# Hybrid attention and retention layer on one core: the row factor of the norm applied after the projections, the turned x split as it is, and two weight panels split twice

## The chip, the cores and the metric

The kernel runs on one core of one Trainium2 chip. Its time is the device time of one execution in microseconds (us), and the figure for a kernel is the median of several executions.

## The reference

One residual layer over x of 2048 rows by 1024 columns: a root-mean-square norm of each row, one input projection whose columns go to window attention and to retention (each with its own gate), one output projection, and the residual.

```
def rms_norm(x, g):
    y = xf * lax.rsqrt(jnp.mean(xf * xf, axis=-1, keepdims=True) + EPS) * g
...
q = rms_norm(q, q_gain); k = rms_norm(k, k_gain)         # window attention, 16 heads, 4 key heads of 64
scores = einsum('bnqhgd,bnkhd->bnhgqk', qb, kb) * scale  # 64 queries, 128 keys, ALiBi bias, sink in the softmax
...
a = einsum('bnihd,bnjhd->bnhij', qc, kc) * dmat          # retention: decay inside a chunk of 64
r = g_chunk * r + s_i                                    # and a state from chunk to chunk
o = (o - mu) * lax.rsqrt(var + EPS)                      # norm of each of 8 heads, then a gain
...
out = x + concat(attn * silu(a_gate), ret * silu(r_gate)) @ w_out
```

The row factor of the first norm, 1/sqrt(mean(x*x) + eps), is one number for each row of x. So it may be multiplied into x before the projections or into their results behind them. The norms of q and k don't care for it, except in their eps, and the norm of the retention heads doesn't either if its eps is scaled.

## The kernel before

**Blocks, units, jobs.** The 2048 rows are 4 blocks of 512 (4 tiles of 128). A block has 4 units, one for each group of 4 query heads with their key head and 2 retention heads, so there are 16 units n = 0 to 15. A unit has 20 projection jobs: 0 to 3 make q, k and v of one tile each (384 columns), 4 and 5 the attention gate, 6 and 7 the retention's q and k, 8 to 11 its v and gate, 12 to 19 the output projection, which runs in the middle of the next unit. Every job fills one of three PSUM banks (jb) in turn. Between the jobs TensorE does small products: TQ (turned q and k), S_ (scores), PT and PV (probabilities), A and I (retention), MT.

**High and low parts.** Each fp32 operand is split into a high part (an fp32r copy) and a low part (what is left), and every product is three matmuls: high by high, low by high, high by low (L1327, L1328, L1329). For the weights ScalarE makes the high part wH from the staging buffer (`wh1`, L508) and GpSimd the low part wL by a subtraction (`wl1`, L360), one slice of 128 rows of a panel at a time. Panels are 0 to 3 in each unit (for jobs 0 to 3, 4 to 7, 8 to 11, 12 to 19) of 8 slices. They are split in block 0 and saved to scratch DRAM (`save`, L204, two DMAs for each pair of slices); blocks 1 to 3 load both parts from there (`reload`, L227). There are 3 staging buffers of a pair of slices.

**x.** The turned x comes from the host (xT) into xt, by tiles of 128 rows. VectorE's `h(b, t)` (L1042) multiplies it by the norm's gain and by the row factor, which TensorE has spread over the partitions (XB, L1443: transposes of xr). ScalarE's `xh` (L648) makes hTH of it, and GpSimd's `xl` (L408), for the first block VectorE's `xl_first` (L804), makes hTL. The row factor is ScalarE's sum of squares of the plain rows (`xsq`, L634), VectorE's `xms_` (L1028) and a power on GpSimd (`xpow`, L401).

**Order.** The order of every engine is written out by hand, unit by unit, as a list of calls; engines wait for one another by semaphores. SyncE issues all DMAs, also in a written order, and a wait in its list holds up every DMA behind it. `carry_in(n)` sets up a unit (negated sinks `nsink` L820, last block's keys and values), `agg` (L914) multiplies the attention gate by its half tanh `ag` (L545), `rpow` (L367) is the power for the norm of q and k.

Of the kernel before, what the change touches and what calls it, by code (L numbers as in the profile page):

```python
# [93 lines left out]
def build(nc, x, norm_gain, q_gain, k_gain, sinks, ret_gain, xT, wp0, wp1, wp2, wp3, c_bias, c_ret, c_ident, out):  # L94
# [9 lines left out]
    with ExitStack() as ctx:  # L104
# [26 lines left out]
        xrb = rawqn_flat[:, 0:BLK]  # L131
# [32 lines left out]
        xss, xms, xr = sb("xss", [P, NT]), sb("xms", [P, NT]), sb("xr", [P, NT])  # L164
# [28 lines left out]
        xbanks = (ptb, ob, ab, sbk)  # L193
# [4 lines left out]
        def _(sp):  # L198
            def save(q):
# [3 lines left out]
                for src, dst in ((wH[b], scrH[n][p]), (wL[b], scrL[n][p])):  # L203
                    sp.dma_start(dst[:, 2 * c:2 * c + 2, :], src[:, 2 * c:2 * c + 2, 0:w].bitcast(F32)).then_inc(s_sv[c], 16)  # L204

            def split(n, p):

                for c in range(4):
# [3 lines left out]
                    sp.dma_start(stage[:, q % STAGES, :, 0:W_WIDTH[p]], wp[p][n, :, 2 * c:2 * c + 2, :]).then_inc(s_w[q % STAGES], 16)  # L212
# [3 lines left out]
            def reload(n, p):  # L216
# [12 lines left out]
            def panel(n, p):  # L229
                if n < NU:  # L230
# [59 lines left out]

# [1323 lines left out]
```

## Time and profile before

| | us |
|---|---|
| median of 3 runs | 1612.38 |
| lowest and highest | 1612.09, 1613.59 |
| the profiled execution, its own time | 1613.94 |
| span of the profile (first to last instruction) | 1612.1 |
| mean granted TensorE clock in the profile | 0.995 |

The profile is of one execution. Its span lies 1.8 us below that execution's own time. Busy time on the five engines stands in the rows below. An engine's idle time costs something only where the end waits for it.

### The profile page before, as it was taken

What the parts mean: (1) busy time and instruction counts of PE and PEld (TensorE: products, weight loads), DVE (VectorE), ACT (ScalarE), POOL (GpSimd) and SP (SyncE); (2) the same over time, 40 slices, a digit from 0 to 9 for tenths busy, and PEclk for the clock granted to TensorE, in tenths of its full rate; (3) what the DMA queues carried; (4) which work ended last, traced back from release to release, by engine and by line L of the source; (5) the groups of instructions that cost most, each with busy time, mean ns of one, the idle gap of its engine ahead of it and who ended that gap; (6) DMA issues with size and microseconds to landing.
All of it is one profiled execution on the core that took longest, in us unless ns stands there. A gap on an engine that the chain in (4) does not pass through costs nothing.

```text
span 1612.1 us, 24573 instructions
## 1 busy us (share of the span) xinstructions
PE 1571.5 (97%) x8208; PEld 1370.7 (85%) x8208; DVE 1139.9 (71%) x3040; ACT 654.8 (41%) x1892; POOL 482.8 (30%) x477
## 2 busy tenths in 40 slices
PE   4999999999899999999999999999999999999998
PEld 4897888988789889898888988889898898988887
DVE  6798686796965757568694775857788575675864
ACT  4655455454433434333443342433343343333430
POOL 4564675655512022120421202122140211202210
PEclk9999999999999999999999999999999999999999
DMA  8776766774855536445357444546356554353451
GB/s 287 263 274 239 273 251 245 261 258 152 302 213 200 195 118 245 159 158 219 126 227 264 176 175 166 187 162 234 133 195 217 188 219 176 121 214 120 182 209 53
DMA packets 123020, 324.67 MB, mean 201 GB/s; under 512 B 16784, under 2 KB 57872, under 8 KB 122896
## 3 DMA queue, kind: packets, MB, share of 16 engines
q1 hardware_dynamic: 122896, 323.10, 55.0%
q8 instruction: 67, 1.10, 0.3%
q14 instruction: 57, 0.47, 0.1%
HBM read 251.75 MB, written 71.30 MB: 200 GB/s over the span
## 4 chain that ended last, share of the span: by engine, by line
PE 78%; DVE 16%; issue 3%; ACT 1%; DMA 1%; POOL 0%; SPq 0%; DVEq 0%; ACTq 0%; POOLq 0%
PE jb L1327 22%; PE jb L1328 22%; PE jb L1329 22%; PE ob L1387 2%; PE ptb L1373 2%; PE s L1364 2%; DVE xt L1042 1%; DVE oraw L1003 1%; PE ob L1346 1%; DVE rawqn L858 1%; DVE qS L867 1%; DVE mixr L931 1%; PE s L1421 1%; DVE rawqn L855 1%; PE s L1422 1%
## 5 line engine op out<-in xcount | busy, mean ns | idle before, releaser
L1327 PE MATMUL jb<-wH,hTH 128*128 128x512 f32 (+1 forms) x1024 | 377.5, 369 | 12.6 <-DVE hTL L804 12.6
L1328 PE MATMUL jb<-wL,hTH 128*128 128x512 f32 (+1 forms) x1024 | 374.2, 365 | 0.0
L1329 PE MATMUL jb<-wH,hTL 128*128 128x512 f32 (+1 forms) x1024 | 373.9, 365 | 0.0
L1327 PEld LDWEIGHTS jb<-wH,hTH 128*128 128x128 f32 x1024 | 194.4, 190 | 32.0 <-DVE hTL L804 12.0
L1329 PEld LDWEIGHTS jb<-wH,hTL 128*128 128x128 f32 x1024 | 194.2, 190 | 20.5
L1328 PEld LDWEIGHTS jb<-wL,hTH 128*128 128x128 f32 x1024 | 194.4, 190 | 18.1
L1327 PE MATMUL jb<-wH,mxH 128*128 128x512 f32 x512 | 208.8, 408 | 0.0
L1327 PE MATMUL jb<-hTH,wH 128*128 128x512 f32 x512 | 201.4, 393 | 0.7 <-POOL wL L360 0.7
L1329 PE MATMUL jb<-wH,mxL 128*128 128x512 f32 x512 | 201.2, 393 | 0.0
L1328 PE MATMUL jb<-wL,mxH 128*128 128x512 f32 x512 | 201.2, 393 | 0.0
L1328 PE MATMUL jb<-hTL,wH 128*128 128x512 f32 x512 | 199.7, 390 | 0.0
L1329 PE MATMUL jb<-hTH,wL 128*128 128x512 f32 x512 | 199.5, 390 | 0.0
L360 POOL TENSOR_TENSOR wL<-stage,wH 128x512 fp32r<-128x512 f32 (+1 forms) x128 | 161.7, 1287 | 73.4 <-ACT wH L508 73.2
L385 POOL TENSOR_TENSOR mxL<-mixr,mxH 128x256 fp32r<-128x256 f32 x64 | 47.2, 737 | 452.8 <-ACT mxH L596 451.7
L551 ACT ACTIVATE sx<-sx,nm 128x128 f32<-128x128 f32 x256 | 99.8, 391 | 191.1 <-DVE d L900 191.1
L367 POOL TENSOR_TENSOR rstd<-ms,mhalf 128x5 f32<-128x5 f32 x64 | 74.9, 1171 | 139.1 <-DVE ms L838 139.1
L1329 PEld LDWEIGHTS jb<-wH,mxL 128*128 128x128 f32 x512 | 96.6, 189 | 21.3
L1329 PEld LDWEIGHTS jb<-hTH,wL 128*128 128x128 f32 x512 | 96.1, 188 | 20.6
L1327 PEld LDWEIGHTS jb<-hTH,wH 128*128 128x128 f32 x512 | 96.2, 188 | 19.6 <-POOL wL L360 1.1
L1328 PEld LDWEIGHTS jb<-hTL,wH 128*128 128x128 f32 x512 | 96.2, 188 | 18.3
L1328 PEld LDWEIGHTS jb<-wL,mxH 128*128 128x128 f32 x512 | 97.1, 190 | 16.6
L1327 PEld LDWEIGHTS jb<-wH,mxH 128*128 128x128 f32 x512 | 96.9, 189 | 16.7
(146 smaller groups left out, 2904.3 us busy)
## 6 DMA issues: line engine op xcount, KB each, us to landing
wH<-scrH SPq DMA_DIRECT2D x144, 512.0 KB, 7.0
wL<-scrL SPq DMA_DIRECT2D x144, 512.0 KB, 7.9
stage<-wp_dram SPq DMA_DIRECT2D x48, 512.0 KB, 6.2
scrH<-wH SPq DMA_DIRECT2D x48, 512.0 KB, 6.1
scrL<-wL SPq DMA_DIRECT2D x48, 512.0 KB, 6.8
wH<-scrH SPq DMA_DIRECT2D x48, 384.0 KB, 5.3
wL<-scrL SPq DMA_DIRECT2D x48, 384.0 KB, 6.6
xt<-xT_dram SPq DMA_DIRECT2D x16, 512.0 KB, 5.9
```

Of the source, the lines that this page charges most:

```text
L360: pool.tensor_tensor(wL[b][:, s, 0:w], stage[:, (at // 2) % STAGES, s % 2, 0:w], wH[b][:, s, 0:w].bitcast(F32), ALU.subtract).then_inc(S[" ...
L367: pool.tensor_tensor(rstd[:, t % 2], ms[:, t % 2], mhalf[:, 0:5], ALU.pow).then_inc(S["s_rstd"], 1)
L385: pool.tensor_tensor(mxL[:, 0:2, cols], mixr[:, :, :], mxH[:, 0:2, cols].bitcast(F32), ALU.subtract).then_inc(S["s_mixl"], 1)
L551: act.activation(v, v, ACT.Exp, bias=nm4[:, t % 2, i:i + 1], accum_out=den[:, t % 2, i:i + 1])
L855: v.tensor_tensor(qn[:, t % 2, 0:320].rearrange("p (h d) -> p h d", d=HD), raw[:, t % 2, 0:320].rearrange("p (h d) -> p h d", d=HD), rstd[ ...
L858: v.tensor_tensor(qn[:, t % 2, 320:384], raw[:, t % 2, 256:320], rstd[:, t % 2, 4:5].broadcast_to([P, HD]), ALU.mult).then_inc(S["s_qn"], 1)
L1327: pe.matmul(o, lh, rh_, start=i == 0, stop=False)
L1328: pe.matmul(o, lh, rl_, start=False, stop=False)
L1329: m = pe.matmul(o, ll, rh_, start=False, stop=i == last)
L1364: m = pe.matmul(s_parts[:, par, hp], qS[:, t % 2, 2 * hp + par], kHL[:, :, win], start=True, stop=True)
L1373: m = pe.transpose(ptb[:, i * P:(i + 1) * P], sx[:, at:at + P], ident[:, :])
L1387: m = pe.matmul(o, v, pT[:, par * 256:(par + 1) * 256].rearrange("p (r q) -> p r q", q=64), start=i == 0, stop=i == 1)
```

## The change

**The row factor goes behind the projections.** ScalarE makes hTH straight from xt times the gain (`xh(b, t, c)`, two of the 8 slices of 128x128 in a call), and VectorE makes hTL = xt*gain - hTH (`xl(b, t, c)`). VectorE's `h` and `xl_first` and GpSimd's `xl` go. The factor xr enters as the scale of ScalarE's copies of q, k, v and of the retention's v and gate, and as a scalar of VectorE's operations on them. The attention gate, whose rows lie along the free axis, gets a new VectorE operation `agz` (gate from bank and xrb) ahead of its tanh; the job that needs the bank next waits for that one. XB(b) is four transposes in a row, needed only by `agz`. `rcur`, a working copy of the retention state, goes too. `carry_in(n)` moves to the end of unit n - 1 (n of 2 and more).

**Two panels are split twice.** Panels 0 and 1 of unit 0 are split in unit 0 as before, but not saved; they are split once more for unit 4 and saved then.

**The start.** The first DMAs come in another order, the first tile of x in four parts, each with its weight chunk; the fourth chunk goes into sx.

```
-SPLITS = [np_ for np_ in PANEL_ORDER if np_[0] < NU]
+LATE = (0,1)
+SPLITS = [(n, p) for n, p in PANEL_ORDER if n < NU or n == NU and p in LATE]
+SAVES = [(n, p) for n, p in SPLITS if n or p not in LATE]
...
+            sp.dma_start(ngain[:, :], norm_gain.rearrange("(k p) -> p k", p=P), allow_slow_non_contiguous=True
+                         ).then_inc(S["s_gains"], 16)
+            for c in range(4):
+                sp.dma_start(xt[:, 0, 2 * c:2 * c + 2], xT[0, 0, :, 2 * c:2 * c + 2]).then_inc(s_xp[c], 16)
+                load(c)
+            x_turned(0, 1)
             first_rows(0)
             sp.dma_start(ident[:, :], c_ident).then_inc(S["s_ident"], 16)
...
+            x_turned(0, 2)
+            first_rows(1)
+            x_turned(0, 3)
+            qk_gains()
+            attention_constants(0)
+            load(4)
             first_rows(2)
+            load(5)
             first_rows(3)
...
-            def h(b, t):
...
-                for k in range(KT):
-                    i = v.scalar_tensor_tensor(out=xt[:, t % 2, k], in0=xt[:, t % 2, k], scalar=ngain[:, k:k + 1],
-                                               in1=factor, op0=ALU.mult, op1=ALU.mult)
...
+            def xl(b, t, c):
+                for k in (2 * c, 2 * c + 1):
+                    v.wait_ge(S["s_xH"], 32 * b + 8 * t + k + 1)
+                    cols = slice(t * P, (t + 1) * P)
+                    v.scalar_tensor_tensor(out=hTL[:, k, cols], in0=xt[:, t % 2, k], scalar=ngain[:, k:k + 1],
+                                           in1=hTH[:, k, cols].bitcast(F32), op0=ALU.mult, op1=ALU.subtract
+                                           ).then_inc(S["s_xL"], 1)
...
+                for k in (2 * c, 2 * c + 1):
+                    act.activation(hTH[:, k, t * P:(t + 1) * P], xt[:, t % 2, k], ACT.Copy, scale=ngain[:, k:k + 1]
+                                   ).then_inc(S["s_xH"], 1)
...
+            def agz(n, i):
+                v.wait_ge(S["s_job"], JOB_DONE[n, J_AG + i])
...
+                v.tensor_tensor(gate[:, i * 512:(i + 1) * 512], bank_of(n, J_AG + i)[:, :], xrb[:, :], ALU.mult
+                                ).then_inc(S["s_agz"], 1)
...
-                    pe.wait_ge(S["s_gate"], nth(m, 2, k - J_AG))
+                    pe.wait_ge(S["s_agz"], nth(m, 2, k - J_AG))
...
-            job(0, 0); job(0, 1); TQ(0, 0); job(0, 2); TQ(0, 1); S_(0, 0); job(0, 3); job(0, 4); TQ(0, 2)
+            job(0, 0); job(0, 1); job(0, 2); job(0, 3); job(0, 4); TQ(0, 0); XB(0); job(0, 5); TQ(0, 1)
```

The orders of ScalarE, VectorE, GpSimd and TensorE are rewritten for units 0 to 4 and little beyond; from unit 5 on only neighbours change places.

ScalarE at the start, before (wH is a weight slice's high part, sx and gate with xss are sums of squares, rawqn from jb is the copy of job (0, 0)):

```order
L634 ACTIVATE gate,xss<-acc 128x1024
L508 ACTIVATE wH<-stage 128x384 x4
L648 ACTIVATE hTH<-xt 128x4x128 x2
L634 ACTIVATE sx,xss<-acc 128x1024
L508 ACTIVATE wH<-stage 128x384 x4
L648 ACTIVATE hTH<-xt 128x4x128 x2
L634 ACTIVATE gate,xss<-acc 128x1024
L516 ACTIVATE rawqn<-jb 128x384
```

and now, from the last slices of panel 0 on:

```order
L532 ACTIVATE wH<-sx 128x384 x2
L678 ACTIVATE hTH<-xt,ngain 128x128 x8
L660 ACTIVATE gate,xss<-acc 128x1024
L678 ACTIVATE hTH<-xt,ngain 128x128 x8
L660 ACTIVATE gate,xss<-acc 128x1024
L678 ACTIVATE hTH<-xt,ngain 128x128 x8
L532 ACTIVATE wH<-stage 128x512 x2
L660 ACTIVATE gate,xss<-acc 128x1024
L540 ACTIVATE rawqn<-jb,xr 128x384
```

The copy of job (0, 0) stood behind the second tile's hTH and the third sum of squares; it now stands behind the hTH of all four tiles, two slices of panel 1 and three sums.

VectorE at the start, before, from the third `xms_` on (kHL and veven with the casts are `carry_in(0)`):

```order
L1028 TENSOR_SCALAR xms<-xss 128x1
L837 TENSOR_REDUCE ss<-th 128x5
L838 TENSOR_SCALAR ms<-ss 128x5
L804 TENSOR_TENSOR vodd<-rawqn,vodd 128x64
L844 CAST veven<-vodd 64x128
L846 CAST veven<-vodd 64x128
L1028 TENSOR_SCALAR xms<-xss 128x1
L1042 SCALAR_TENSOR_TENSOR xt<-xt,ngain,ab 128x128 x8
L855 TENSOR_TENSOR rawqn<-rawqn,rstd 128x320
L858 TENSOR_TENSOR rawqn<-rawqn,rstd 128x64
L820 TENSOR_SCALAR nsink<-sink 128x2
L821 CAST kHL<-kcar 128x2x64
```

and now, from its first operation behind the memsets on:

```order
L1092 SCALAR_TENSOR_TENSOR hTL<-xt,ngain,hTH 128x128 x16
L1085 TENSOR_SCALAR xe<-xss 128x1
L1085 TENSOR_SCALAR xm<-xss 128x1 x2
L1092 SCALAR_TENSOR_TENSOR hTL<-xt,ngain,hTH 128x128 x8
L858 TENSOR_SCALAR nsink<-sink 128x2
L859 CAST kHL<-kcar 128x2x64
L860 CAST veven<-vcar 64x128
L1085 TENSOR_SCALAR xe<-xss 128x1
L1085 TENSOR_SCALAR xm<-xss 128x1 x2
L1092 SCALAR_TENSOR_TENSOR hTL<-xt,ngain,hTH 128x128 x8
L1085 TENSOR_SCALAR xe<-xss 128x1
L1085 TENSOR_SCALAR xm<-xss 128x1 x2
```

The wait for the sinks (`nsink`) stood behind the first q and k; it now stands between the low parts of the third and of the fourth tile of x.

GpSimd at the end of unit 3, before (hTL is the next block's x):

```order
L385 TENSOR_TENSOR mxL<-mixr,mxH 128x2x128
L393 TENSOR_TENSOR gg<-gg,gain 128x256
L408 TENSOR_TENSOR hTL<-xt,hTH 128x4x128 x2
L393 TENSOR_TENSOR gg<-gg,gain 128x256
L408 TENSOR_TENSOR hTL<-xt,hTH 128x4x128 x2
L385 TENSOR_TENSOR mxL<-mixr,mxH 128x2x128
```

and now:

```order
L387 TENSOR_TENSOR wL<-stage,wH 128x384 x2
L412 TENSOR_TENSOR mxL<-mixr,mxH 128x2x128
L387 TENSOR_TENSOR wL<-stage,wH 128x384 x3
L420 TENSOR_TENSOR gg<-gg,gain 128x256
L387 TENSOR_TENSOR wL<-stage,wH 128x384 x3
L420 TENSOR_TENSOR gg<-gg,gain 128x256
L412 TENSOR_TENSOR mxL<-mixr,mxH 128x2x128
```

The low parts of x have gone to VectorE, and the eight slices of unit 4's panel 0 stand in their place; its panel 1 follows in unit 4.

## Rows read from the trace of the kernel before

**Rows 1.** The page's busy times, shares of the span and instruction counts.

```profile
PE 1571.5 (97%) x8208; PEld 1370.7 (85%) x8208; DVE 1139.9 (71%) x3040; ACT 654.8 (41%) x1892; POOL 482.8 (30%) x477
```

**Rows 2.** TensorE's waits: tile, line, releaser: us in total, times, longest.

```profile
PE jb L1327 <- DVE hTL L804: 12.6, 3, 5.7
PE ob L1346 <- DVE kHL L872: 9.9, 8, 3.7
PE ptb L1443 <- POOL xr L401: 6.4, 1, 6.4
```

**Rows 3.** Windows: length, busy us (instructions) by engine, granted clock, DMA share, GB/s.

```profile
0.00:26.00 26.00, 12.38 (x52) 11.47 (x53) 16.19 (x44) 14.13 (x29) 11.87 (x18) 1.00 0.78 260
26.00:54.00 28.00, 19.13 (x82) 17.16 (x83) 22.41 (x51) 12.27 (x33) 14.51 (x11) 0.82 0.85 324
54.00:147.00 93.00, 89.46 (x482) 77.99 (x481) 82.51 (x191) 55.17 (x154) 54.88 (x49) 1.00 0.74 260
147.00:400.00 253.00, 250.49 (x1301) 215.91 (x1300) 190.42 (x461) 130.32 (x351) 146.26 (x132) 1.00 0.65 236
400.00:440.00 40.00, 33.40 (x179) 30.41 (x178) 38.31 (x97) 15.36 (x41) 23.84 (x20) 0.91 0.81 302
440.00:1600.00 1160.00, 1158.69 (x6086) 1011.53 (x6085) 787.50 (x2198) 427.51 (x1289) 231.46 (x248) 1.00 0.50 183
```

**Rows 4.** Windows around two stretches of low clock, same columns.

```profile
29.00:35.80 6.80, 3.76 (x12) 3.76 (x13) 6.20 (x13) 2.30 (x4) 5.06 (x4) 0.50 1.05 408
431.80:438.60 6.80, 5.09 (x14) 4.15 (x15) 6.49 (x20) 1.31 (x3) 1.77 (x2) 0.50 1.03 347
```

**Rows 5.** Timeline of the start: start us, duration us, engine, line, operation, [idle before].

```profile
2.12 0.43 SPq L294 DMA_DIRECT2D ngain<-norm_gain_dram  x1
...
7.36 2.16 DVE L1042 SCALAR_TENSOR_TENSOR xt<-xt,ngain,ptb 128x128 f32<-128x128 f32 x8 [1.86 <-DMA ngain<-norm_gain_dram]
8.42 1.99 ACT L508 ACTIVATE wH<-stage 128x384 fp32r<-128x384 f32 x4 [3.18 <-DMA stage<-wp_dram]
9.02 4.32 POOL L360 TENSOR_TENSOR wL<-stage,wH 128x384 fp32r<-128x384 f32 x4 [2.80 <-ACT wH L508]
...
12.54 0.69 PE L1327 MATMUL jb<-wH,hTH 128*128 128x384 f32 x1 [5.73 <-DVE hTL L804]
```

**Rows 6.** Timeline, 24 to 54 us.

```profile
24.08 1.29 SPq L262 DMA_DIRECT2D sink<-sink_logits_dram  x2
...
29.50 0.17 DVE L820 TENSOR_SCALAR nsink<-sink 128x2 f32<-128x2 f32 x1 [3.65 <-DMA sink<-sink_logits_dram]
...
32.04 0.69 PE L1327 MATMUL jb<-wH,hTH 128*128 128x384 f32 x1 [5.58 <-DVE hTL L804]
...
53.44 0.50 PE L1327 MATMUL jb<-hTH,wH 128*128 128x512 f32 x1 [0.70 <-POOL wL L360]
```

**Rows 7.** Groups of one shape: line, engine, count | busy us, mean ns | idle before.

```profile
L367 POOL TENSOR_TENSOR rstd<-ms,mhalf 128x5 f32<-128x5 f32 x64 | 74.9, 1171 | 139.1 <-DVE ms L838 139.1
...
L360 POOL TENSOR_TENSOR wL<-stage,wH 128x384 fp32r<-128x384 f32 x32 | 33.9, 1084 | 2.8 <-ACT wH L508 2.8
...
L408 POOL TENSOR_TENSOR hTL<-xt,hTH 128x512 fp32r<-128x512 f32 x24 | 31.5, 1334 | 0.0
...
L1042 DVE SCALAR_TENSOR_TENSOR xt<-xt,ngain,rawqn 128x128 f32<-128x128 f32 x96 | 28.3, 366 | 0.0
...
L940 DVE TENSOR_TENSOR th<-jb,cret 128x512 f32<-128x512 f32 x16 | 11.0, 690 | 30.0 <-PE jb L1329 30.0
...
L804 DVE TENSOR_TENSOR hTL<-xt,hTH 128x512 fp32r<-128x512 f32 x8 | 8.0, 1032 | 1.6 <-ACT hTH L648 1.4
```

**Rows 8.** Timeline of VectorE, 396 to 412 us.

```profile
396.32 2.19 DVE L1042 SCALAR_TENSOR_TENSOR xt<-xt,ngain,rawqn 128x128 f32<-128x128 f32 x8
...
405.50 4.27 DVE L1042 SCALAR_TENSOR_TENSOR xt<-xt,ngain,rawqn 128x128 f32<-128x128 f32 x8
```

**Rows 9.** Timeline of GpSimd inside the second of these.

```profile
406.38 2.72 POOL L360 TENSOR_TENSOR wL<-stage,wH 128x512 fp32r<-128x512 f32 x2
```

More of the change, by code:

```diff
@@ L289, in first_rows, with qk_gains, load @@
                 sp.dma_start(acc[:, t], x[0, t * P:(t + 1) * P, :]).then_inc(s_first[t], 16)
+            def qk_gains():
+                for half in range(2):
+                    rows = slice(half * HD, half * HD + HD)
+                    sp.dma_start(qkg[rows, 0:1], q_gain.rearrange("(d o) -> d o", o=1)).then_inc(S["s_qkg"], 16)
+                    sp.dma_start(qkg[rows, 1:2], k_gain.rearrange("(d o) -> d o", o=1)).then_inc(S["s_qkg"], 16)
+            def load(q):
+                (n, p), c = SPLITS[q // 4], q % 4
+                if q >= STAGES + 1:
+                    sp.wait_ge(S["s_wl"], 2 * (q - STAGES) + 2)
+                sp.dma_start(stage_of(q, W_WIDTH[p]), wp[p][n, :, 2 * c:2 * c + 2, :]).then_inc(s_stage(q), 16)
@@ L312, in _ @@
-            attention_constants(0)
-            panel(0, 1)
+            load(6)
+            load(7)
+            for q in range(5):
+                sp.wait_ge(S["s_wl"], 2 * q + 2)
+                save(q)
             retention_constants(0)
@@ L399, in xpow @@
             def xpow(b, t):
+                if b >= 2:
+                    pool.wait_ge(S["s_mr"], 16 * (b - 1))
                 pool.wait_ge(S["s_xms"], nth(b, 4, t))
[L401 to L409 removed]
@@ L977, in rupd @@
                     rows = slice(a * 64, a * 64 + 64)
-                    new = rcur[rows, :] if t < NT - 1 else rst[rows, u:u + 1].rearrange("p o c -> p (o c)")
-                    i = v.scalar_tensor_tensor(out=new, in0=rcur[rows, :], scalar=cg[rows, :],
+                    i = v.scalar_tensor_tensor(out=rst[rows, u], in0=rst[rows, u], scalar=cg[rows, :],
                                                in1=sbk[rows, a * P:(a + 1) * P], op0=ALU.mult, op1=ALU.add)
@@ L1047, in xl_first @@
-            def xl_first(t):
-                for half in range(2):
-                    v.wait_ge(S["s_xH"], 2 * t + half + 1)
-                    ks, cols = slice(4 * half, 4 * half + 4), slice(t * P, (t + 1) * P)
-                    sub(hTL[:, ks, cols], xt[:, t % 2, ks], hTH[:, ks, cols]).then_inc(S["s_xL"], 1)
-            xms_(0, 0); h(0, 0); xl_first(0); xms_(0, 1); h(0, 1); xl_first(1); xms_(0, 2)
-            qk_stats(0, 0); v_parts(0, 0); xms_(0, 3); h(0, 2); qk_norm(0, 0); carry_in(0); qk_stats(0, 1)
@@ new lines, in _ @@
+            xl(0, 0, 0); xl(0, 0, 1); xl(0, 0, 2); xl(0, 0, 3); xl(0, 1, 0); xl(0, 1, 1); xl(0, 1, 2)
+            xl(0, 1, 3); xms_(0, 0); xl(0, 2, 0); xl(0, 2, 1); xl(0, 2, 2); xl(0, 2, 3); carry_in(0); xms_(0, 1)
+            xl(0, 3, 0); xl(0, 3, 1); xl(0, 3, 2); xl(0, 3, 3); xms_(0, 2)
+            qk_stats(0, 0); v_parts(0, 0); xms_(0, 3); qk_stats(0, 1); qk_norm(0, 0); v_parts(0, 1)
+            qk_norm(0, 1); qk_stats(0, 2); v_parts(0, 2); qk_stats(0, 3); v_parts(0, 3); qk_norm(0, 2)
+            tql(0, 0); agz(0, 0); agg(0, 0); agz(0, 1); qk_norm(0, 3); tql(0, 1); part1(0, 0); agg(0, 1)
```

873 lines of the change are left out of this document (439 added, 434 removed).

## The prediction

> **What bounds the kernel now.** I read the page's busy times first. TensorE is busy for 1571.5 of 1612.1 us [rows 1], so 40.6 us is all that it can win by waiting less, and the change leaves its own work as it is. Its list of waits says which engine it waits for: VectorE. Most of it is for the low part of x (12.6 us) and the q and k of a tile (9.9), and 6.4 us go before the row factor xr of the first tile is there [rows 2]. The table of windows says when. From 440 to 1600 us TensorE idles 1.3 us of 1160 [rows 3]: nothing can be won there, and VectorE, with 372 us of rest, can take more work. The rest of the idle time lies in four stretches: 13.6 us up to 26 us, 8.9 from there to 54, 3.5 up to 147, and 6.6 from 400 to 440, where the next block's x is made; 147 to 400 holds 2.5 [rows 3]. After its idle times TensorE also ran at the lower clock. In 29 to 35.8 us and 431.8 to 438.6 the granted clock was 0.50, the level of 1.2 GHz, behind waits of 5.6 and 3.7 us [rows 2, 4, 6]. At half clock half of the busy 3.8 and 5.1 us is the clock's: 1.9 and 2.5 us, and the window 26 to 54 with a mean of 0.82 has it once more.
>
> What must be seen beside this is how busy VectorE is in the same windows. In 54 to 147 us it works 82.5 of 93, in 400 to 440 it works 38.3 of 40 [rows 3]. In these two it, not TensorE, sets the pace; a lead that TensorE brings into them is kept only so far as VectorE has room.
>
> **The start, up to job (0, 4).** Before, the first job waited for the chain plain rows, sum of squares, xr, XB, `h`, `xh`, `xl_first`: it began at 12.54 [rows 5]. Now it needs a quarter of xt, the gains and one weight chunk. The gains were issued at 2.12 and waited for until 7.36, so 5.2 us [rows 5]; issued first, near 0.7, they land near 5.9. The first weight chunk was there at 8.42 [rows 5]; 1.0 MB (the plain rows and the xt tile) no longer goes ahead of it, so I put it below 7. ScalarE's two `xh` of 128x128 and one `wh1` follow (a pair of slices took 1.0 by rows 5, an `xh` is smaller), and GpSimd starts near 7.0 instead of 9.02. It then paces TensorE: 8 slices at 1.084 [rows 7] are 8.7, so job (0, 0) ends at 15.7, or up to 17.5 where VectorE's low parts get in its way. Jobs (0, 1) and (0, 2) of 24 matmuls each follow until about 25.
>
> Then comes the wait that replaces the one removed. Job (0, 3) needs `xl(0, 3)`, and this stands on VectorE behind `carry_in(0)`, whose `nsink` needs the sinks. These were issued at 24.08 and waited for until 29.50 [rows 6], 5.4 us. Now twenty DMAs stand ahead of them, the last tile of x waiting for `xl(0, 1)` near 18; with 0.6 us for each of the seven small ones (1.29 for two, rows 6) the sinks are issued near 22 and land near 27.4. ScalarE's copy of job (0, 0), which frees the bank, also stands behind two slices of panel 1 and the third sum of squares, whose DMAs are issued after the sinks. So job (0, 3) starts at 29 to 31, after an idle time of 5 us, and as before the clock is low behind it. That is no loss against before: there the job after the wait was the third (32.04 [rows 6]), here it is the fourth.
>
> Job (0, 4) needs panel 1, and GpSimd paces it from about 27: eight slices of 512 columns at about 1.3 (in proportion from 1.084 for 384, and 2.72 for two in rows 9) are 10.9, three `rpow` at 1.17 [rows 7] and two `xpow` make 15. It ends at 44.5. Before, it ended near 54.4 [rows 6], with some 2.8 us of TQ and S_ done that now come later. TensorE is ahead by 54.4 - 2.8 - 44.5 = 7, with bounds of 5 and 8.5.
>
> **What VectorE lets through.** Its own ledger up to 54 us: gone are 32 `h` for 8.6 (343 ns each while their factor came from PSUM), `xl_first` for 8.0 [rows 7] and `rcur`. New are 32 `xl` at no less than 0.27 (2.19 for eight, rows 8), so 8.7; three instead of one `xms_`, 0.6; two `agz` at 0.69 (the nearest row is the 128x512 from bank and table, rows 7), 1.4. That would leave it 6 us ahead. But `xl` reads xt and hTH from SBUF, and there the trace shows a price. Eight such operations took 2.19 us at 396.32 with GpSimd idle, and 4.27 at 405.50 with two of GpSimd's subtractions running through them [rows 8, 9]: 1.0 us for each subtraction that meets them. Eight to ten do so at the start (GpSimd has no pause there), 8 to 10 us; the same with PSUM as a source cost nothing. The bounds are 0 and 10. So VectorE comes to 54 us with a lead between -4 and 6, and can besides shed some of its 10.5 us of rest in 54 to 147 [rows 3], most of which is waits in a chain with ScalarE. Of TensorE's 7 I take half: **3.5 us**, with bounds of 0 and 11 (7 plus the 3.5 idle in 54 to 147).
>
> The Trainium skill states in its GPSIMD Engine Reference, in the table Specifications, that GpSimd's SBUF interfaces are shared with VectorE and contend with VectorE's instructions that have two SBUF inputs. By that rule every `xl` beside a `wl1` is slowed, and so are `agg`, whose bank operand has become SBUF, and the new gate; the trace agrees by the 4.27 against 2.19. The skill's page DMA: Bandwidth & Descriptors (Bandwidth, Measured) calls transfers under 64 KB descriptor-dominated; by its fit of 2.0 us plus bytes the gains would land 3 us earlier than with the 5.2 that rows 5 show, and the start would win that much more until panel 1 paces it.
>
> **The seam of block 1 (unit 3 into 4).** Before, VectorE had 32 `h` of 0.27 to 0.53, and GpSimd 8 `xl` at 1.334 [rows 7], 10.7 us. Now VectorE has 32 `xl` of the same size, GpSimd no `xl` but 16 more slices at 1.08 to 1.36, about 19.5 us, of which the eight of panel 0 lie beside the `xl`. What goes is the chain: XB, xrb and `h` before anything can be split; now ScalarE makes hTH as soon as the jobs of unit 3 free it, and VectorE follows. TensorE's loss there was 6.6 idle and 2.5 of low clock, 9.1 in all. VectorE at 38.3 of 40 has no reserve, it loses `rcur` and gains `agz` of 0.7 each. I take **5**, with bounds of 0 and 9.
>
> **Elsewhere.** Seams of units 1 to 3: `agz` 6 at 0.7 on a VectorE that is nearly full, contention for `agg`, against 2.5 us idle to win [rows 3] and a `carry_in` that now stands ahead of the next unit's first q and k, for which TensorE waited longest but for x (9.9 in eight waits, rows 2): a gain of **1**, bounds a gain of 2.5 and a loss of 4. From 440 on 24 `agz`, 17 us, and 64 `xl` lie on a VectorE with 372 us of rest, under a TensorE that is never waiting: 0, and 1.3 could be won; were that cover gone, each `agz` would put 0.7 between a job and its bank. The 16 reloads that become eight stage loads: 0, reloads are issued long ahead. The end of the program is unchanged.
>
> **Sum.** 3.5 + 5 + 1 is 9.5 less, against the profiled execution's 1613.9 (span 1612.1 and 1.8 around it), so 1604.4; the median lies 1.5 below that execution, so **1603**.
>
> **The rivals.**
> - *VectorE isn't the limit* (0.22). Contention stays near 0, its rests in 54 to 147 close, and TensorE keeps all: 8.5 + 3.5 at the start, 9 at the seam, 1 elsewhere are 22 at the far end, 7 + 6 + 1 are 14 at the near: 1590 to 1598. For it speaks that 7 us is ahead early and that the list of waits shows single waits of a chain, not a steady queue; against it 38.3 of 40.
> - *The start's lead is lost again* (0.18). ScalarE's and VectorE's lists wait together for the late small DMAs, and VectorE comes to 54 us behind. Then only the seams are won, 6 less, or 2 if the latter goes badly too: 1606 to 1611.
> - *The subtractions block the split* (0.06). If half of the 32 `xl` before unit 4 each meet one of GpSimd's slices, at 1.0 us each that is 16 us on a VectorE with 1.7 us of rest, of which 2 were paid before too: 12.3 more for job (4, 0) to wait in place of 5 less, so with the other two terms 7.8 over before, 1620. It is slower than can be told from no change with 12 blocked ones. Against it: eight slices of panel 0, not 16, stand there, and they come with gaps.
> - *It does nothing* (0.04): the start's wait moves from 12.5 and 32 to 29 and the seam's to another tile, 1611 to 1613.
>
> **How the numbers follow.** The main case holds 0.50, 1598 to 1607. The range leaves out the far quarter of the first rival, the last of the second and the two small ones, some 2 in 10: 1592 to 1610. About 0.2% (3.2 us) is what a measurement can tell. Faster than 1609.2 are the main case, the first rival and about half of the second: 0.81. Slower than 1615.6 is the third with a little for what I don't see, 0.07. The rest is 0.12.
>
> **What would show it.** The first projection matmul starts near 8 us; TensorE stands from 25 to 29 or 31 before the copy's bank or hTL; `nsink` waits for the sinks near 27; panel 1's last subtraction is near 43.5. VectorE's `xl` has a mean near 0.5 at the start and beside panel 0 of unit 4. In 54 to 147 TensorE still has a few us idle with VectorE near 9 tenths; between 400 and 440 the wait of 3.7 us is gone or short. Wrong would be: an `agz` that PE waits for in the steady part, an idle time there over 5 us, or a seam with waits for hTL over 4 us.

## The result and the profile after

The changed kernel took 1620.39 us (median of 5 runs, 1617.99 to 1621.99), the kernel before 1612.38 (median of 5, 1611.72 to 1613.59): a ratio of 1.0049 with a 95% interval of 1.0039 to 1.0060. It is slower by 8 us, where 9.5 us less were forecast. The profiled execution took 1619.3 us, with a span of 1617.5, which is 5.4 more than before.

The page's busy times of the changed kernel:

```profile
PE 1576.1 (97%) x8208; PEld 1373.7 (85%) x8208; DVE 1177.6 (73%) x3080; ACT 701.8 (43%) x2005; POOL 474.6 (29%) x469
```

TensorE executes the same 8208 matmuls and is busy 4.6 us longer than in [rows 1]. The lower clock (0.992 in the mean, 0.995 before) accounts for that: 0.003 of 1617 us is 4.9. Its idle time grew only from 40.6 us to 41.4. Its waits, as in [rows 2]:

```profile
PE jb L1376 <- POOL wL L387: 9.7, 4, 7.6
PE ob L1395 <- DVE kHL L909: 9.4, 3, 4.4
PE jb L1376 <- ACT rawqn L540: 5.7, 1, 5.7
PE ob L1395 <- DVE rawqn L895: 3.9, 3, 2.1
...
PE jb L1376 <- DVE gg L999: 2.8, 1, 2.8
```

The waits for x are gone, and so is the one for the row factor. The waits for kHL (the keys and queries of a tile, at the end of a chain over q and k) were 9.9 us before and are 9.4 now, but they come as three, two of them 4.4 us long, where there were eight of at most 3.7. The first matmul now waits for GpSimd's first slice (7.6 of the 9.7 us for wL) and job (0, 3) for ScalarE's copy of q and k (rawqn, 5.7); waits for two banks (acc and gg) are new. By stage, against [rows 3]:

```profile
0.00:26.00 26.00, 16.01 (x72) 14.21 (x72) 16.38 (x41) 16.80 (x45) 9.74 (x15) 1.00 0.69 219
26.00:54.00 28.00, 22.48 (x99) 18.88 (x100) 21.41 (x48) 19.73 (x42) 27.11 (x22) 0.88 0.63 226
54.00:147.00 93.00, 86.00 (x444) 74.96 (x443) 85.24 (x200) 53.78 (x157) 49.46 (x45) 0.94 0.68 250
147.00:400.00 253.00, 244.25 (x1258) 211.27 (x1257) 198.85 (x437) 132.90 (x352) 143.90 (x130) 0.99 0.62 229
400.00:440.00 40.00, 36.83 (x209) 33.61 (x208) 38.49 (x108) 23.25 (x63) 20.38 (x20) 1.00 0.68 263
440.00:1600.00 1160.00, 1157.19 (x6076) 1010.04 (x6075) 813.31 (x2247) 455.32 (x1347) 223.97 (x241) 1.00 0.51 185
```

Up to 54 us TensorE did 38.5 us of work instead of 31.5: the start is better by 7. From 54 to 400 us it idled 15.8 us, where before it idled 6.1, and the clock fell to 0.94 in the first of these stretches, where it had been 1.00.

The jobs are the same in both kernels and in the same order, so their ends can be laid side by side. Job ends in us, read from the last matmul of each job:

```
end of job   before   changed   difference
(0, 0)         19.9      15.5      -4.5
(0, 4)         54.4      44.4     -10.1
(1, 1)        113.4     102.8     -10.5
(1, 2)        117.5     111.6      -5.9
(0, 16)       143.0     142.8      -0.2
(2, 0)        209.1     208.6      -0.5
(1, 15)       238.4     243.3      +4.8
(2, 15)       337.4     346.4      +9.0
(4, 0)        407.9     415.4      +7.5
(4, 4)        464.6     471.4      +6.8
(15, 3)      1505.5    1511.0      +5.4
```

Between the jobs TensorE does small products, and their places moved too. Up to the end of job (0, 4) the changed kernel has done 2 of their matmuls and the kernel before 16; up to (1, 1) it is 102 against 115, up to (0, 16) 150 against 151. So the table shows the lead too large up to (1, 1), by 1.7 us there: in work done it is near 9 us.

So there are three stories. The start wins 10 us by this table. The seam of unit 1 (jobs (1, 2) to (0, 16)) takes all of it back. These 10.3 us are 1.7 for the small products, 3.8 more of idle time (7.0 instead of 3.3), and the rest, near 5, is low clock: 0.81 from 102.8 to 111.6 us and 0.82 from 125 to 142.8, where the kernel before had 1.00. The seams of units 2 and 3 lose 8 more between jobs (2, 0) and (4, 0), 5.3 in the first up to job (1, 15). From job (4, 5) on, where the changed kernel is 7.3 us behind, it wins 1.9 us up to the end.

**The start**, in the timeline of the changed kernel: the first matmul, the wait for the sinks on VectorE, job (0, 3) behind the copy that frees its bank, and job (0, 4) behind a slice of panel 1.

```profile
7.56 0.69 PE L1376 MATMUL jb<-wH,hTH 128*128 128x384 f32 x1 [7.56 <-POOL wL L387]
...
24.80 0.17 DVE L858 TENSOR_SCALAR nsink<-sink 128x2 f32<-128x2 f32 x1 [5.89 <-DMA sink<-sink_logits_dram]
...
29.49 0.69 PE L1376 MATMUL jb<-wH,hTH 128*128 128x384 f32 x1 [5.69 <-ACT rawqn L540]
...
43.39 0.50 PE L1376 MATMUL jb<-hTH,wH 128*128 128x512 f32 x1 [1.68 <-POOL wL L387]
```

**The seam of unit 2.** VectorE between 225 and 238 us, of which the operations on q and k and one cast are shown (L892 and L895 multiply q and k by their factor, L875 makes the mean square, L885 is a cast of v, L904 and L909 end the chain):

```profile
225.03 1.45 DVE L892 TENSOR_TENSOR rawqn<-rawqn,rstd 128x320 f32<-128x320 f32 x1
226.40 1.30 DVE L895 TENSOR_TENSOR rawqn<-rawqn,rstd 128x64 f32<-128x64 f32 x1
...
229.98 1.30 DVE L875 TENSOR_SCALAR ms<-ss 128x5 f32<-128x5 f32 x1
...
232.72 1.22 DVE L885 CAST vcar<-vodd 64x128 fp32r<-64x128 f32 x1
233.96 1.47 DVE L892 TENSOR_TENSOR rawqn<-rawqn,rstd 128x320 f32<-128x320 f32 x1
235.35 1.28 DVE L895 TENSOR_TENSOR rawqn<-rawqn,rstd 128x64 f32<-128x64 f32 x1
236.66 0.98 DVE L904 SCALAR_TENSOR_TENSOR qS<-ob,qkg,qS 64x256 fp32r<-64x256 f32 x2
237.66 0.35 DVE L909 SCALAR_TENSOR_TENSOR kHL<-ob,qkg,kHL 128x128 fp32r<-128x128 f32 x1
```

and GpSimd at the same time:

```profile
224.83 2.79 POOL L387 TENSOR_TENSOR wL<-stage,wH 128x512 fp32r<-128x512 f32 x2 [1.26 <-ACT wH L532]
...
229.98 1.29 POOL L387 TENSOR_TENSOR wL<-stage,wH 128x512 fp32r<-128x512 f32 x1
231.43 1.17 POOL L394 TENSOR_TENSOR rstd<-ms,mhalf 128x5 f32<-128x5 f32 x1 [0.17 <-DVE ms L875]
232.57 6.44 POOL L387 TENSOR_TENSOR wL<-stage,wH 128x512 fp32r<-128x512 f32 x5
```

Read the two together. Six operations of VectorE that take their tensors from SBUF meet a slice on GpSimd and end about when a slice does: 1.45, 1.30, 1.30, 1.22, 1.47, 1.28. L904 and L909, which read a bank (ob), run under the same slices in the 0.98 and 0.35 that they take elsewhere. The same place in the kernel before:

```profile
225.53 0.49 DVE L855 TENSOR_TENSOR rawqn<-rawqn,rstd 128x320 f32<-128x320 f32 x1
225.94 0.22 DVE L858 TENSOR_TENSOR rawqn<-rawqn,rstd 128x64 f32<-128x64 f32 x1
...
230.90 1.50 DVE L855 TENSOR_TENSOR rawqn<-rawqn,rstd 128x320 f32<-128x320 f32 x1
232.32 1.31 DVE L858 TENSOR_TENSOR rawqn<-rawqn,rstd 128x64 f32<-128x64 f32 x1
...
234.66 0.35 DVE L872 SCALAR_TENSOR_TENSOR kHL<-ob,qkg,kHL 128x128 fp32r<-128x128 f32 x1
```

There the first pair took 0.49 and 0.22 and only the second pair was held. The changed list puts two slices of panel 1 ahead of gpow (the power for the norm of the retention heads). A third stands between gpow and the last rstd in both lists, but before it ran at 226.79, ahead of the mean square. Now the first pair (2.0 us longer), the mean square (1.1) and the cast (1.0) are held as well. Other changes of VectorE's list give some of that back, and kHL is ready 3.0 us later, at 237.66 instead of 234.66. TensorE waits 4.4 us there instead of 0.8.

One part of this has a second reading. The power rstd at 231.43 stands behind the third slice in GpSimd's own list, and that slice ended at 231.27; so it could hardly have started earlier even with a short mean square. Here GpSimd's queue alone would have given nearly the same delay, and no run separates the two. The lengths of the other held operations are VectorE's own and leave no such doubt.

**The seam of unit 1.** Job (1, 2) needs the bank of job (0, 11), which `rvg(0, 3)` frees (the copies of v and gate out of the bank; gg is its last). VectorE:

```profile
94.29 2.24 DVE L977 TENSOR_TENSOR mixr<-rawqn,gate 64x256 f32<-64x256 f32 x2
...
100.38 1.51 DVE L843 TENSOR_TENSOR aL<-amr,aH 128x256 fp32r<-128x256 f32 x1
...
102.52 2.20 DVE L977 TENSOR_TENSOR mixr<-rawqn,gate 64x256 f32<-64x256 f32 x2
...
105.15 0.41 DVE L999 SCALAR_TENSOR_TENSOR gg<-th,jb 128x256 f32<-128x256 f32 x1
```

and on GpSimd, five slices of panel (0, 3) in a row:

```profile
97.75 6.68 POOL L387 TENSOR_TENSOR wL<-stage,wH 128x512 fp32r<-128x512 f32 x5
```

ScalarE had its part of `rvg(0, 3)` done at 95.25; VectorE came to it at 104.75. The pair mixr took 2.24 and 2.20 us here and 0.85 at 492.56, where no slice ran; aL took 1.51 instead of 0.41.

### The profile page after: what moved, and what is told of

It is laid out like the page before. It is cut to its first block, busy times and chain, and to the rows that moved or that the text cites. A ratio compares the mean times of both kernels' runs of the same rounds, so it can differ in the third digit from the quotient of the medians.

```text
span 1617.5 us, 24760 instructions
## 1 busy us (share of the span) xinstructions
PE 1576.1 (97%) x8208; PEld 1373.7 (85%) x8208; DVE 1177.6 (73%) x3080; ACT 701.8 (43%) x2005; POOL 474.6 (29%) x469
## 4 chain that ended last, share of the span: by engine, by line
PE 88%; DVE 7%; issue 1%; POOL 1%; DMA 1%; SPq 1%; ACT 0%; ACTq 0%; DVEq 0%; POOLq 0%
PE jb L1376 25%; PE jb L1377 25%; PE jb L1378 25%; PE ob L1434 2%; PE s L1411 2%; PE ptb L1420 2%; PE ob L1395 1%; PE s L1466 1%; PE s L1467 1%; DVE rawqn L895 1%; PE s L1469 1%; PE ab L1479 1%; DVE hTL L1092 1%; DMA stage<-wp_dram 1%; PE s L1312 1%
## 5 line engine op out<-in xcount | busy, mean ns | idle before, releaser
L387 POOL TENSOR_TENSOR wL<-stage,wH 128x512 fp32r<-128x512 f32 (+1 forms) x142 | 178.1, 1280 | 65.6 <-ACT wH L532 65.4
```

Source lines behind the costliest of these rows:

```text
L387: pool.tensor_tensor(wL[b][:, s, 0:w], stage_of(at // 2, w)[:, s % 2], wH[b][:, s, 0:w].bitcast(F32), ALU.subtract).then_inc(S["s_wl"], 1)
```

## The experiments

Theory A is that GpSimd's subtractions, placed beside VectorE's work on SBUF, hold it up where TensorE waits for it. Its rivals put the loss on VectorE's own order or its amount of work. A third explanation, that the powers come late in GpSimd's own list because slices stand ahead of them, was given no run of its own. All ratios below are to the kernel before on the same chip. Differences to the changed kernel are against its 1620.39 us; the kernel before took 1612.38 beside it and 1612.25 to 1612.30 beside the runs below.

**1. The order of the slices in the seams of units 2 and 3, back and forth.** First in the changed kernel (GpSimd; on ScalarE `wh1(2, 1, 0)` and `wh1(3, 1, 0)` go behind ocopy and mth likewise):

```
-rpow(2, 2); wl1(2, 1, 0); wl1(2, 1, 1); gpow(1, 3); wl1(2, 1, 2); rpow(2, 3); wl1(2, 1, 3)
+rpow(2, 2); gpow(1, 3); wl1(2, 1, 0); rpow(2, 3); wl1(2, 1, 1); wl1(2, 1, 2); wl1(2, 1, 3)
...
-rpow(3, 2); wl1(3, 1, 0); wl1(3, 1, 1); gpow(2, 3); wl1(3, 1, 2); rpow(3, 3); wl1(3, 1, 3)
+rpow(3, 2); gpow(2, 3); wl1(3, 1, 0); rpow(3, 3); wl1(3, 1, 1); wl1(3, 1, 2); wl1(3, 1, 3)
```

> The changed kernel, with GpSimd's and ScalarE's order of the kernel before at two places, in units 2 and 3: the first slices of panel 1 (wh1, wl1) stand behind the GroupNorm power gpow and, but for one, behind the power of the last q and k again. Theory A (a slice's subtraction on GpSimd holds up VectorE's multiplication of q and k by their factor, which TensorE waits for): the two idle times of 4.8 us at 233 and 337 us, with the low clock behind them, go; 8 to 10 us less than the changed kernel, so 1611 to 1613. Rival B (VectorE's own new order and the moved carry_in make q and k late; the slices don't matter): within 1.5 us of the changed kernel, 1619 to 1622.

Measured: 1617.21 us, ratio 1.0028 (1.0018 to 1.0037), 3.2 us less than the changed kernel; in the two profiles 4.6 us of span. The wait for kHL fell to 5.3 us in all. The first pair took 0.49 and 0.22 again, but the mean square was still held (1.31) by the one slice that stands between gpow and rpow. Right in sign, a third of the size.

The same in the kernel before, the other way round, shown for unit 2:

```
-rpow(2, 2); gpow(1, 3); wl1(2, 1, 0); rpow(2, 3); wl1(2, 1, 1); wl1(2, 1, 2); wl1(2, 1, 3)
+rpow(2, 2); wl1(2, 1, 0); wl1(2, 1, 1); gpow(1, 3); rpow(2, 3); wl1(2, 1, 2); wl1(2, 1, 3)
...
-xsq(1, 2); qkv(2, 2); xsq(1, 3); ocopy(1, 3); tqh(2, 0); mth(1, 1); qkv(2, 3); wh1(2, 1, 0)
-wh1(2, 1, 1); wh1(2, 1, 2); wh1(2, 1, 3); tqh(2, 1); rh(2, 0); mth(1, 2); wh1(2, 1, 4); wh1(2, 1, 5)
+xsq(1, 2); qkv(2, 2); xsq(1, 3); ocopy(1, 3); tqh(2, 0); mth(1, 1); wh1(2, 1, 0); wh1(2, 1, 1)
+qkv(2, 3); wh1(2, 1, 2); wh1(2, 1, 3); tqh(2, 1); rh(2, 0); mth(1, 2); wh1(2, 1, 4); wh1(2, 1, 5)
...
```

> The kernel before, with nothing of the change but this: in units 2 and 3 the first two slices of panel 1 go ahead of gpow and of the last q and k, as in the changed kernel. Theory A: TensorE's waits for kHL appear there, 3 to 5 us each with the clock behind them, 6 to 10 us slower than before: 1618 to 1622. Rival B: within 1 us of before, 1611.5 to 1613.5.

Measured: 1616.30 us, ratio 1.0023 (1.0014 to 1.0033): the order alone costs the kernel before 4 us. In its profile each of the two seams lost 1.3 us, since one operation more was held (L858, 1.32 instead of 0.22). That is neither A's full size nor rival B's nothing.

**2. The same orders, but short subtractions.** GpSimd subtracts only 64 of a slice's columns in all panels but those of unit 0, so this leaves out part of the weights' low parts. TensorE's work, the transfers and all orders stay.

```
+                w = w if n == 0 else 64
```

> The changed kernel, where GpSimd's subtraction for the weights takes only the first 64 columns of a slice in all panels but those of unit 0 (the rest of wL keeps old values, so part of the low parts is left out). TensorE's work, all transfers and all orders stay. Theory A (the losses between 150 and 460 us are GpSimd's subtractions meeting VectorE): these losses go, 10 to 14 us less than the changed kernel, 1606 to 1610, and less than the kernel before with the same edit. Rival B (VectorE's order or its own work): the times at 233 and 337 us stay, no more than 4 us less, 1616 to 1620.

> The kernel before with the same edit: GpSimd's subtraction takes 64 columns of a slice in all panels but those of unit 0, so part of the low parts is left out. Theory A: before loses less to them, 2 to 6 us less than before, 1606 to 1610, and the changed kernel with this edit is level with it or faster. Rival B: 0 to 2 us less than before, and the changed kernel with this edit stays 5 to 9 us behind it.

Measured: changed kernel 1592.71 us, ratio 0.9873 (0.9859 to 0.9888); kernel before 1594.66, ratio 0.9890 (0.9875 to 0.9905). Both gained far more than expected: 27.7 us and 17.6. Their difference of 10 us is more than the 8 us by which the change had lost. Without long slices the changed kernel is 2 us ahead. Theory A's direction held and its sizes (10 to 14 and 2 to 6) did not. Rival B, which wanted it 5 to 9 us behind, is out. But the lead was still small: of 8.8 us at job (1, 1), 1.5 were left at job (0, 16). Panels 2 and 3 of unit 0 were full here.

**3. Short subtractions in unit 0 too.** Full are only its panels 0 and 1; panel 2 has 128 of 512 columns, panel 3 has 64.

```
+                o = slice(0, w) if n == 0 and p < 2 else slice(384, 512) if (n, p) == (0, 2) else slice(0, 64)
```

> The changed kernel with GpSimd's subtraction thin in unit 0 as well: 128 of 512 columns in its panel 2, 64 in its panel 3 and in all panels of later units; only its panels 0 and 1 are full (so part of the low parts is left out). Theory A1 (the lead of 10 us at job (0, 4) is lost to slices that meet VectorE in the first unit): the lead over the kernel before with the same edit stays at 7 us or more up to job (0, 16), 1586 to 1590. Rival F (the lead is empty, VectorE's own list starts its attention part 9 us later than before and is full up to the end of unit 1, slices or not): the lead is still gone to 3 us or less by job (0, 16), 1590 to 1593.

> The kernel before with the same edit (128 of 512 columns in unit 0's panel 2, 64 in its panel 3 and in all panels of later units, so part of the low parts is left out). Both theories: within 3 us under the version whose unit 0 is full (1594.7), 1591 to 1595. A1 wants it at least 5 us above the changed kernel with this edit, rival F within 3.

Measured: changed 1588.96 us, ratio 0.9855 (0.9841 to 0.9870); before 1595.79, ratio 0.9897 (0.9882 to 0.9911). The difference is now 6.8 us for the change. Windows of the changed kernel with this edit:

```profile
44.00:147.00 103.00, 101.95 (x551) 89.58 (x551) 85.68 (x226) 66.73 (x189) 32.34 (x58) 1.00 0.70 258
147.00:400.00 253.00, 253.00 (x1336) 221.72 (x1335) 176.61 (x494) 139.82 (x378) 76.17 (x133) 1.00 0.65 241
```

TensorE idles 1.1 us from job (0, 5) on up to 147 us, and nothing up to 400. VectorE works 85.7 of the 103 us, where in the changed kernel it works 93.7, and 176.6 in the second window instead of 198.9, with TensorE further on in the program: so at least 22 us of its busy time there were waiting. The lengths of single operations say it more directly. In this second window of the changed kernel 47 of VectorE's 436 operations took over 0.15 us longer than the median of their form, 40 us in sum. GpSimd was at work under every one of them, on a weight slice under 45. With the short slices it was 11 of 494 and 4 us; the kernel before has 33 of 460 and 29 us.

The 8.6 us of lead at job (1, 1) are still 8.6 at job (1, 2), and 5.8 at (0, 16). At job (1, 1) the lead is the same with panel 2 full or short, and its slices end by 56 us in the changed kernel, so it is panel 3 of unit 0 that cost most of the start's lead. Of the 2.8 us that still go, 1.1 is one wait of TensorE for VectorE (acc), and the other 1.7 are TensorE's own: 13 more matmuls of small products stand in this stretch in the changed order. Rival F (VectorE's own list) is left with 1.1 at most. Theory A1 wanted a lead of 7 us or more at (0, 16) and rival F one of 3 or less; 5.8 lies between. A1's time for the changed kernel and its distance of at least 5 us held, and the kernel before came out 0.8 above its range.

**4. What the second split costs and saves.** All panels saved in unit 0, none split in unit 4:

```
-LATE = (0,1)
+LATE = ()
...
-rkl(3); wl1(4, 0, 0); wl1(4, 0, 1); mixl(3, 2); wl1(4, 0, 2); wl1(4, 0, 3); wl1(4, 0, 4); ggm(3, 0)
+rkl(3); mixl(3, 2); ggm(3, 0)
```

> The changed kernel without its second split: panels 0 and 1 of unit 0 are saved when they are split, and unit 4 loads them; the 16 slices of unit 4 are gone on ScalarE and GpSimd, everything else stands. Theory A (slices on GpSimd beside VectorE's work are the cost): the seam of unit 4 loses its waits of 4 us and the ones behind it, 4 to 7 us less than the changed kernel, 1613 to 1616. Rival C (the 16 saves back in the first 50 us hold up the loads of panel 2 behind them, which the second split avoided): the start gives back 3 us or more, 1618 to 1622.

Measured: 1624.18 us, ratio 1.0068 (1.0051 to 1.0084): 3.8 us slower than the changed kernel, so theory A's sum was wrong. Rival C had the right direction, and 2.2 us too little at the top of its range. The timeline of SyncE, ScalarE and TensorE in this kernel:

```profile
43.46 0.50 SPq L225 DMA_DIRECT2D stage<-wp_dram  x1
...
49.94 1.15 ACT L532 ACTIVATE wH<-stage 128x512 fp32r<-128x512 f32 x2 [12.42 <-DMA stage<-wp_dram]
...
57.62 0.87 PE L1395 MATMUL ob<-ident,rawqn 128*128 128x128 f32 x3 [5.46 <-DVE kHL L909]
```

Ten saves of panels 0 and 1 stand ahead of panel 2's first load, which is issued at 43.46 instead of 35.60. ScalarE waits 12.4 us for it, ahead of the copy of q and k. Job (0, 8) ends 8.8 us later. Behind it both halves of A's thought are there too: from job (4, 3) to job (5, 4) this kernel gains 3.5 us on the changed one, since its 16 slices are gone. The second split is worth 9 at the start and costs 3.5 in unit 4. The two profiled executions are 5.2 us apart, as these two numbers want; the medians only 3.8.

**5. The one bank.** `rvg(0, 3)` earlier in VectorE's list:

```
-rupd(0, 1); gna(0, 1); kwl_al(0, 2); mix(0, 3); rvg(0, 3); kw_am(0, 3); rl(0, 2); gnv(0, 1)
+rupd(0, 1); gna(0, 1); rvg(0, 3); kwl_al(0, 2); mix(0, 3); kw_am(0, 3); rl(0, 2); gnv(0, 1)
```

> The changed kernel, with rvg(0, 3), which frees the bank of job (0, 11), ahead of kwl_al(0, 2) and mix(0, 3) in VectorE's list, as nothing else. Theory A (the start's lead of 10 us is lost because VectorE's list is behind by then, and TensorE waited for this one bank): job (1, 2) starts 3 to 4.6 us earlier, and if VectorE's remaining work doesn't take it back in unit 1, the end comes 3 to 4.6 us earlier, 1616 to 1617. Rival D (VectorE is the limit in the whole of unit 1, whichever order it takes): the wait only moves to the next q and k, under 1.5 us, 1619 to 1621.

Measured: 1619.25 us, ratio 1.0042 (1.0029 to 1.0055), 1.1 us less than the changed kernel, within its scatter. Theory A's 3 to 4.6 us did not come. Job (1, 2) ended 4.2 us earlier, job (0, 16) 1.7 earlier and job (4, 4) 1.0 later: the seams took it back. That is rival D's size, though by experiment 3 it isn't the amount of VectorE's work that did it.

**6. Slices wait for q and k.** In the changed kernel GpSimd begins panel 1 of units 1 to 4 only when the last q and k of the unit are scaled:

```
-rpow(2, 2); wl1(2, 1, 0); wl1(2, 1, 1); gpow(1, 3); wl1(2, 1, 2); rpow(2, 3); wl1(2, 1, 3)
+rpow(2, 2); gpow(1, 3); rpow(2, 3); wl1(2, 1, 0); wl1(2, 1, 1); wl1(2, 1, 2); wl1(2, 1, 3)
...
+                if n and p == 1 and s == 0:
+                    pool.wait_ge(S["s_qn"], nth(n, 4, 3))
```

> The changed kernel, where GpSimd begins with panel 1 of units 1 to 4 only when VectorE has scaled the last q and k of the unit (a wait for qk_norm(n, 3) and the order rpow, gpow, rpow, slices). Theory A: no slice of panel 1 meets the scaling of q and k in any seam; the kHL waits of 9.4 us and their low clock go, 9 to 13 us less than the changed kernel, 1607 to 1611. Rival E (the slices only move to other work of VectorE, and the loads of panels 1 and 2 come late): 0 to 4 us less, or a new wait of TensorE for wL, 1616 to 1621.

Measured: 1609.72 us, ratio 0.9985 (0.9976 to 0.9994): 10.7 us less than the changed kernel, from one wait and four places in a list. In its profile VectorE's last pair in unit 2 and GpSimd behind it:

```profile
227.59 0.49 DVE L894 TENSOR_TENSOR rawqn<-rawqn,rstd 128x320 f32<-128x320 f32 x1
228.00 0.22 DVE L897 TENSOR_TENSOR rawqn<-rawqn,rstd 128x64 f32<-128x64 f32 x1
...
228.36 10.03 POOL L389 TENSOR_TENSOR wL<-stage,wH 128x512 fp32r<-128x512 f32 x8 [1.14 <-DVE rawqn L897]
```

Both pairs are short, and the wait for kHL fell from 9.4 us to 1.3. From job (2, 0) to (1, 15) this kernel takes 28.3 us, as long as with short slices; the changed kernel took 34.7 and the kernel before 29.3. But rival E had a part too. The eight slices now meet other work (an operation of the softmax, d, took 1.21 us at 233.46). From job (1, 15) to (3, 0) this kernel takes 72.1 us instead of 69.0, with 1.9 us of waits for mixr, acc and kHL, and 3.3 us more go from (2, 15) to (4, 0). So about half of what the two seams gained (6.4 and 5.9 us) was lost again behind them.

The same wait in the kernel before, in units 1 to 3:

> The kernel before with the wait alone: panel 1's slices of units 1 to 3 behind the last scaling of q and k. Theory A: it loses less to them than the changed kernel did, since its waits for kHL in units 1 to 3 are under 1 us each apart from one of 2.6; 1 to 3 us less than before, 1609 to 1611.5. If it comes out above 1612.5, the wait does harm of its own (late loads of panel 1).

Measured: 1612.25 us, ratio 0.9999 (0.9990 to 1.0009), no change where 1 to 3 us less were expected. Its long wait for kHL, 3.7 us in unit 4, stands where it stood, and the short ones had cost little.

**7. Together.** First with the second split left out as well (planned before its own result was known):

> The three edits together in the changed kernel: no second split, rvg(0, 3) first, and panel 1's slices of units 1 to 3 behind the last scaling of q and k. Theory A: the savings add, with the start's lead kept: 1598 to 1606, under the kernel before. Rival: they overlap, since each gives back only what VectorE's list loses again: 1608 to 1613.

Measured: 1616.17 us, ratio 1.0022 (1.0013 to 1.0032). Theory A wanted 1598 to 1606 and the rival 1608 to 1613, and both missed. It carries the 9 us of experiment 4: job (0, 8) ends at 78.9. Then experiments 5 and 6 with the second split kept:

> The changed kernel with both edits that gave something: panel 1's slices of units 1 to 4 behind the last scaling of q and k, and rvg(0, 3) first. With the second split kept, since leaving it out cost 3.8 us. Theory A (adding up: 10.7 and what rvg(0, 3) gave before unit 1's seam took it back): 1604 to 1608. Rival F (VectorE is full up to the end of unit 1, so that the second edit gives nothing): 1609 to 1611.

Measured: 1608.36 us, ratio 0.9974 (0.9963 to 0.9985). That lies between the two ranges. It beats both kernels, by 12 us the changed one and by 3.9 the one before; against experiment 6 alone the 1.4 us less are within the scatter of the runs. What is left in its list of waits:

```profile
PE jb L1378 <- POOL wL L389: 10.6, 6, 7.6
PE jb L1378 <- DVE acc L1080: 7.3, 5, 3.2
PE jb L1378 <- ACT rawqn L542: 5.7, 1, 5.7
PE ob L1397 <- DVE kHL L911: 4.0, 3, 2.3
```

The first row is mostly the start itself (7.6 us up to the first matmul), the second is `add` (a result added to acc, which frees its bank) in the seams of units 1 to 4. It was 3.5 us in the changed kernel.

## Why the prediction was wrong

The forecast added three gains: 3.5 us at the start, 5 in the seam of block 1, 1 elsewhere. Read from the two profiles, the change gained 0.2 up to job (0, 16) and 0.3 from there to (2, 0), lost 8.0 from (2, 0) to (4, 0), gained 0.7 up to (4, 4) and 1.4 up to the end: 5.4 lost. The medians are 8.0 apart: the profiled execution lies 1.6 us above the median in the kernel before and 1.1 below it in the changed one.

**The start up to job (0, 4)** was right. The first matmul came at 7.56 (near 8 was said), TensorE stood from 23.8 to 29.49 before job (0, 3) (25 to 29 or 31) and waited for the bank that ScalarE's copy frees. Job (0, 4) ended at 44.4 (44.5). The gains took 2.4 us from issue to landing, not the 5.2 of [rows 5], with nothing issued ahead of them. By that row alone the start was put too late, and it was worth little, because ScalarE's table load ran until 5.1 us. The 2.4 us are nearer to the fit of 2.0 us plus bytes on the Trainium skill's page DMA: Bandwidth & Descriptors than to the row that I took; that page made its fit from transfers that GpSimd issues, and these were issued by SyncE.

**"Of TensorE's 7 I take half"** was the first step that failed. TensorE's 7 us were there at 54 us in full (38.5 us of work done instead of 31.5). It kept them up to job (1, 1), and between there and job (0, 16) the job ends lost 10.3. The cost was booked where VectorE's `xl` would meet slices, which is up to 54 us; it came at the next place where both lists were dense, 93 to 143 us, on other operations (mixr 2.2 instead of 0.85, aL 1.5 instead of 0.4). Experiment 3 shows that 7.5 of these 10.3 go with the slices, with the low clock behind the waits; 1.7 are moved products. The 0.2 left stand against 3.5 forecast; 0 was within the bounds of this term.

**"Elsewhere: a gain of 1, bounds a gain of 2.5 and a loss of 4"** was the step that turned the sign. From job (2, 0) to (4, 0) the change lost 8.0 us. I read the diff of GpSimd's list for units 2 and 3 as an exchange of neighbours. It moved two slices of 1.3 us ahead, and with the third they came among the operations that TensorE's chain over q and k hangs on. The price of one slice (1.0 us for an operation that meets it, [rows 8, 9]) was in hand; it was applied to `xl` and, without a number, to `agg`, and not to q and k. Experiment 1 gives back 4.2 of these 8.0 us and experiment 6 gives back 5.9, so the place of the slices is the cause of most of it.

**"The seam of block 1: 5"** rested on a wrong cause. The 3.7 us wait for kHL before [rows 2] was put down to the chain xrb, `h`, split. But with short slices it is gone from the kernel before without any part of the change, and the kernel gains 6.3 us at job (3, 13). In the kernel before GpSimd

```profile
424.36 2.99 POOL L360 TENSOR_TENSOR wL<-stage,wH 128x512 fp32r<-128x512 f32 x2
```

held VectorE's pair in the same way:

```profile
424.62 1.58 DVE L855 TENSOR_TENSOR rawqn<-rawqn,rstd 128x320 f32<-128x320 f32 x1
426.12 1.31 DVE L858 TENSOR_TENSOR rawqn<-rawqn,rstd 128x64 f32<-128x64 f32 x1
```

In the changed kernel no wait for kHL is left in this seam, and up to job (3, 13) it had gained 6.0 us, more than the 5 forecast. From there to job (4, 4) it lost 5.3. TensorE waits 2.9 us there (2.0 of them for acc), the clock is 0.85 from 440.7 to 452 us, and slices of unit 4's panel 1 run on GpSimd; without them (experiment 4) the same stretch lost 2.4. That leaves 0.7. The term left out what the new slices cost in the second half of the seam.

**From 440 us on** 0 was forecast, and 1.9 us were won from job (4, 5) on, near 1.0 around the seam of each of the two later blocks; what gives it is open. `agz` took 0.69 us as assumed, and TensorE never waited for it. The prediction counted the new gate among what slices slow, but `agz` reads one of its two inputs from a bank, and no `agz` took over 0.69. None of the three signs of being wrong came: they watched `agz`, the steady part and hTL, and the loss was in q and k.

**The rivals.** The third, "the subtractions block the split", with 0.06, named the mechanism and by its sum even the time, 1620. That the time fits is luck, since its place was wrong. At the start `xl` had a mean of 0.49 us, near the 0.5 that was said, with 7 of 32 held, and in unit 3 four of 32 were held, not half. What cost TensorE its time were the scaling of q and k and the mix. The first rival, that VectorE isn't the limit, is true only with short slices (experiment 3).

## What to carry to other kernels

VectorE's busy share is no measure of its work where GpSimd runs beside it: 40 of 199 us in one stretch here were waiting inside its own instructions. Look for one form of instruction with two durations (0.22 and 1.30) before you call an engine full. When a long GpSimd operation changes its place in a list, write down what stands beside it on VectorE, and for which of these TensorE waits; a wait that keeps it off that chain pays if its result is needed late, but look at what it meets in its new place (here about half of the gain of a seam). A wait of the kernel before is a term of the forecast only once its own cause is known.

## What the runs showed that was not expected

- A subtraction of 128x512 on GpSimd holds VectorE's operations with one tensor as input as well: the mean square on 128x5 took 1.30 us instead of 0.17, while its slice took 1.29. The Trainium skill's GPSIMD Engine Reference (Specifications) names instructions with two SBUF inputs and those in a 2-port mode, and the runs agree with the first kind; whether this one ran in such a mode, no row tells.
- The loss isn't proportional: two slices of a seam moved ahead cost the kernel before 1.3 us. In the changed kernel the same seam lost 5.3 (up to job (1, 15)), and moving the two back returned 2.0 of it. There the slices held an early and a late link of one chain, and the clock was 0.85 behind the wait (232 to 243.3 us).
- Shortening GpSimd's subtractions alone, which TensorE nearly never waits for, took 17.6 us off the kernel before, more than all its waits for kHL (9.9, [rows 2]). In the two profiles TensorE's idle time fell by 11.8 us and its busy time by 7.5, at a clock of 0.998 instead of 0.995.
